# Moving the gate of a mixer's output projection onto its weights, and splitting its last half by columns

## The reference

```python
mix = jnp.concatenate([h_m, h_a], axis=-1) @ w_out[l]
x = x + gate1 * mix
hn2 = rms_norm(x, g_norm2[l]) * (1.0 + scale2) + shift2
ffn = hierarchical_moe(hn2, ...)      # route to 2 of 32 experts, SwiGLU, d_expert 512
x = x + gate2 * ffn
```

## Time and profile before

| what | us |
|---|---|
| median of 3 runs | 1333.73 (1332.79 to 1334.61) |
| the profiled execution | 1333.06 |
| its span from first to last instruction | 1331.1 |
| PE busy in the span | 1307.8 (98%), 7862 matmuls |
| DVE busy | 791.4 (59%) |
| ACT busy | 566.0 (43%) |
| POOL busy | 33.7 (3%), 55 instructions |
| DMA | 371.83 MB, mean 279 GB/s |
| granted TensorE clock, mean over the span | 0.997 of full |

### The profile page before, as it was taken

The page is one execution under the profiler, slowest core; times in us unless marked ns, Lnnn a source line. Parts: engine busy times, 40 slices in busy tenths (PEclk is TensorE's granted clock), DMA queues, the critical chain, the costliest instruction groups (busy, mean ns, idle before and its releaser), DMA issues.

```text
span 1331.1 us, 19341 instructions
## 1 busy us (share of the span) xinstructions
PE 1307.8 (98%) x7862; PEld 970.2 (73%) x7862; DVE 791.4 (59%) x1397; ACT 566.0 (43%) x859; POOL 33.7 (3%) x55
## 2 busy tenths in 40 slices
PE   8999999999999999999999999999999999999997
PEld 8988789999887997999987888754444544444442
DVE  5755598888986655898896877743222222223213
ACT  5344545655546576666655746531111111111112
POOL 0200010000001000100010000000000000000000
PEclk9999999999999999999999999999999999999998
DMA  9467286767585742555765573599999999999995
GB/s 354 165 222 259 103 301 218 237 216 252 196 290 176 236 147 95 170 191 187 253 226 190 206 253 127 190 398 412 427 429 427 429 428 428 428 426 429 426 423 204
DMA packets 113373, 371.83 MB, mean 279 GB/s; under 512 B 4604, under 2 KB 64284, under 8 KB 100368
## 3 DMA queue, kind: packets, MB, share of 16 engines
q1 hardware_dynamic: 105648, 344.07, 67.1%
q0 software_dynamic: 7648, 26.72, 5.7%
HBM read 369.71 MB, written 1.05 MB: 279 GB/s over the span
## 4 chain that ended last, share of the span: by engine, by line
PE 86%; DMA 7%; DVE 4%; ACT 2%; SPq 1%; issue 1%; DVEq 0%; ACTq 0%
PE ps L673 15%; PE ps L1588 14%; PE ps L633 9%; PE ps L634 9%; PE ps L635 9%; PE ps L1611 7%; PE ps L1570 4%; PE ps L650 4%; PE ps L652 3%; PE ps L651 3%; DMA arena<-in_w_expert_gate_dram 3%; DMA arena<-in_w_expert_down_dram 3%; PE ps L1617 2%; DVE w_low L568 1%; DMA const<-in_const_dram 1%; PE ps L1262 1%
## 5 line engine op out<-in xcount | busy, mean ns | idle before, releaser
L568 DVE TENSOR_TENSOR w_low<-ring,w_high 128x1024 fp32r<-128x1024 f32 x264 | 311.5, 1221 | 98.4 <-ACT w_high L560 97.6
L560 ACT ACTIVATE w_high<-ring 128x1024 fp32r<-128x1024 f32 x264 | 264.9, 1052 | 177.9 <-PE ps L673 82.8
L633 PE MATMUL ps<-h_high,w_high 128*128 128x256 f32 x1088 | 310.4, 285 | 1.6 <-DVE h_low L472 1.4
L634 PE MATMUL ps<-h_low,w_high 128*128 128x256 f32 x1088 | 307.8, 283 | 0.0
L635 PE MATMUL ps<-h_high,w_low 128*128 128x256 f32 x1088 | 307.7, 283 | 0.0
L633 PEld LDWEIGHTS ps<-h_high,w_high 128*128 128x128 f32 x1088 | 208.6, 192 | 7.2 <-issue 5.2
L634 PEld LDWEIGHTS ps<-h_low,w_high 128*128 128x128 f32 x1088 | 208.7, 192 | 0.0
L635 PEld LDWEIGHTS ps<-h_high,w_low 128*128 128x128 f32 x1088 | 208.6, 192 | 0.0
L1588 PE MATMUL ps<-ring,arena 128*64 128x512 f32 x592 | 176.6, 594 | 2.2 <-DMA arena<-in_w_expert_gate_dram 1.7
L1588 PEld LDWEIGHTS ps<-ring,arena 128*64 128x64 f32 x592 | 56.3, 137 | 111.6 <-issue 111.5
L673 PE MATMUL ps<-w_high,h_high 128*128 128x512 f32 x304 | 95.0, 394 | 1.0 <-DVE arena L2373 0.9
(11 more groups left out here) (402 smaller groups left out, 1682.5 us busy)
## 6 DMA issues: line engine op xcount, KB each, us to landing
ring<-in_ffn_w_up_dram SPq DMA_DIRECT2D x44, 1024.0 KB, 7.6
ring<-in_w_expert_gate_dram SPq DMA_DIRECT2D x19, 2048.0 KB, 23.1
ring<-in_w_expert_up_dram SPq DMA_DIRECT2D x18, 2048.0 KB, 19.6
ring<-in_w_expert_down_dram SPq DMA_DIRECT2D x17, 2048.0 KB, 24.2
ring<-in_ret_w_in_dram SPq DMA_DIRECT2D x11, 2048.0 KB, 8.2
arena<-in_w_expert_up_dram SPq DMA_DIRECT2D x11, 2048.0 KB, 25.7
ring<-in_ffn_w_down_dram SPq DMA_DIRECT2D x10, 2048.0 KB, 8.3
arena<-in_w_expert_gate_dram SPq DMA_DIRECT2D x9, 2048.0 KB, 21.1
```

The source lines that it names most:

```text
L560: nc.scalar.activation(hi, raw, ACT.Copy).then_inc(hi_done, 1)
L568: last = eng.tensor_tensor(lo, raw, hi.bitcast(F32), ALU.subtract)
L633: nc.tensor.matmul(o, hi, hTh[:, k, :], start=(k == 0 if whole else n == 0), stop=False, skip_group_check=not whole)
L634: nc.tensor.matmul(o, hi, hTl[:, k, :], start=False, stop=False, skip_group_check=not whole)
```

## The change

The gate is multiplied into `w_out` in its ring slots by GpSimd, eight multiplications of 128x1024, in place, float32. Two of them (`pool_done`) release the high split of each half of `mix_out` on ACT. The residual is then one addition PSUM plus x per column half. In the last half of `mix_out`, tile 1 is multiplied by column halves: all six matmuls of column half 0, a signal (`tile0_mm` once more), then the six of column half 1. The scratch tile `gtmp` goes. The semaphore `ada_zero` is renamed and shared.

```diff
@@ split_high
             if m >= 2:
                 act.wait_ge(wide_mm, (m - 1) if i is None else i * per + (m - 1))
+            if phase == "mix_out":
+                act.wait_ge(pool_done, 2 + h + 1)
@@
+        def by_columns(pe, h, w):
+
+            for half in range(2):
+                for kc in range(2):
+                    hi, lo = (s[:, 2 * (h % 4) + kc, P:T] for s in (hTh, hTl))
+                    for a, b, c in ((hi, 0, 0), (hi, 1, 1), (lo, 0, 2)):
+                        cols = slice(kc * D + half * C, kc * D + (half + 1) * C)
+                        last = nc.tensor.matmul(ps[:, 6 + half, :], a, w[b][:, cols], start=False, stop=(kc == 1 and c == 2))
+                if half == 0:
+                    last.then_inc(tile0_mm, 1)
+            return last
@@ project
                 for t in range(NT):
                     if t and middle is not None:
                         middle(h)
+                    if t and phase == "mix_out" and h == n - 1:
+                        last = by_columns(pe, h, w)
+                        continue
@@
-        def gated_residual(link, g, bank, tmp, tiles):
-
-            for t in tiles:
-                for half in range(2):
-                    last = nc.vector.tensor_tensor(tmp[:, t, half * C:(half + 1) * C], ps[:, bank + 2 * t + half, :],
-                                                   gates[:, g, half * C:(half + 1) * C], ALU.mult)
-            link(last)
-            for t in tiles:
-                nc.vector.tensor_tensor(x[:, t, :], x[:, t, :], tmp[:, t, :], ALU.add).then_inc(x_new, 2)
@@ end of GpSimd's program
+            pool.wait_ge(ada_gate, 4)
+            for n in phases["mix_out"]:
+                slot = units[n][1]
+                pool.wait_ge(ring_in[slot], arrivals(n))
+                for k in range(4):
+                    gated = nc.gpsimd.tensor_tensor(tall[slot][:, k, :], tall[slot][:, k, :], gates[:, 0, :], ALU.mult)
+                    if k % 2:
+                        gated.then_inc(pool_done, 1)
@@ VectorE's program
             for t in range(NT):
-                if t == 0:
-                    dve.wait_ge(tile0_mm, len(PROJECTIONS))
-                    wide_done(dve, n_halves - 1)
-                else:
-                    wide_done(dve, n_halves)
-                dve.wait_ge(ada_gate, 4)
-                gated_residual(link, 0, 4, gtmp, (t,))
+                for half in range(2):
+                    if t == 0 and half == 0:
+                        dve.wait_ge(tile0_mm, len(PROJECTIONS))
+                        wide_done(dve, n_halves - 1)
+                    elif t == 1:
+                        dve.wait_ge(*((wide_mm, n_halves) if half else (tile0_mm, len(PROJECTIONS) + 1)))
+                    xs = x[:, t, half * C:(half + 1) * C]
+                    nc.vector.tensor_tensor(xs, ps[:, 4 + 2 * t + half, :], xs, ALU.add).then_inc(x_new, 1)
```

More of the change, by code:

```diff
@@ L747, in build @@
         perm_in = sem("perm_in")
-        ada_used, ada_ev, ada_zero, ada_mods, ada_ms, mods_in, ada_gsum, ada_gate, ada_c, bias_in = (
-            sem("ada_" + n) for n in ("used", "evicted", "zero", "mods", "mods_row", "mods_in", "gate_sum", "gate", "c",
+        ada_used, ada_ev, pool_done, ada_mods, ada_ms, mods_in, ada_gsum, ada_gate, ada_c, bias_in = (
+            sem("ada_" + n) for n in ("used", "evicted", "pool_done", "mods", "mods_row", "mods_in", "gate_sum", "gate", "c",
                                       "bias_in"))
@@ L836, in build @@
         selw = carve(896, NT, P)
-        gtmp = carve(1408, NT, D)
         xg = carve(1408, KD, P)
@@ L1067, in _ @@
             pool.wait_ge(x_new, update(2))
-            nc.gpsimd.memset(w8, 0.0).then_inc(ada_zero, 1)
-            pool.wait_ge(ada_zero, 2)
+            nc.gpsimd.memset(w8, 0.0).then_inc(pool_done, 1)
+            pool.wait_ge(pool_done, 2)
             pool.dma_start(w8[:, :, 0:8], A["w_in_2"][0].rearrange("(k p) n -> p k n", p=P)[:, :, 4 * LH * LDH:4 * LH * LDH + 8])\
@@ L1757, in _ @@
             vg_group(3, ACT.Silu, False)
-            act.wait_ge(ada_zero, 1)
+            act.wait_ge(pool_done, 1)
             act.wait_ge(small_in, 32)
@@ L2142, in _ @@
             link = Link(dve, dve_chain)
-            nc.vector.memset(hT[:, 0, :], 0.0).then_inc(ada_zero, 1)
+            nc.vector.memset(hT[:, 0, :], 0.0).then_inc(pool_done, 1)
             split_low(dve, "ret_qk", 0)
```

## The result

| | before | changed |
|---|---|---|
| median of 6 runs, us | 1334.11 (1332.79 to 1336.42) | 1343.49 (1342.79 to 1344.45) |
| span of the profiled execution, us | 1331.1 | 1341.7 |
| DVE busy, us | 791.4 | 801.5 |
| POOL busy, us | 33.7 | 54.7 |

The ratio is 1.0074, 95% interval 1.0064 to 1.0084: the changed kernel is slower by 8.5 to 11.2 us, 9.4 by the medians and 10.6 by the two spans. The forecast was +5.8 us and 1339.5, with a range up to 1343.8.

A forecast was written before the change was run, and what follows sets the result against it. The end was taken to be set by the expert-weight stream's restart, delayed by the PE, DVE, ACT chain before it. Terms -0.4 + 6.2 = +5.8 us on the median 1333.73 gave 1339.5 us, range 1332.9 to 1343.8.

The forecast's parts named there:

- The 2.0 us of tile 1: Residual at the end of `mix_out`: tile 1's x ready 2.0 us sooner, but nobody waits for it, so no gain.
- Rival C: DVE and POOL don't exclude each other; only the 0.4 us wait at the first transpose goes: 1333.3 us, chance 0.24.
- B: DVE and POOL exclude each other, but the room takes it: 0 to 2.7 us late, 1333.5 to 1336, chance 0.12.
- D: Faster: all DVE time removed would be on the path, 2.5 us, giving 1331.3 us; chance 0.04.
- Part 1, -0.4 us,: Residual at the mixer's end: tile 0's x comes sooner, PE's wait goes, and the end gains -0.4 us.
- The wait of 0.4 us: At PE's first transpose: its weight load waited 0.4 us for DVE's tile 0 addition; this would go whole.
- Part 4, +6.2 us,: POOL's multiplications and DVE's work in `mix_out` hold each other off, making the kernel +6.2 us slower.
- The middle of two orders: POOL against DVE's low splits: the middle of alternate turns (8 us) and DVE keeping its turn (4 us), +6.2 us.
- the walk: Step-by-step timing of DVE's low splits, halves 11 to 13, against POOL's 2.4 us operations: PE stands 8 us in all.
- The split of half 13 has 3 us of room.: POOL's last two operations meet half 13's split and the gated rows behind it: between 0 and 1 us more.

The follow-up runs named there:

- e1: The changed kernel without GpSimd's eight multiplications and ACT's wait for them, gate left out: 1332.85 us against 1333.25 for the kernel before, ratio 0.9998.
- e7: The changed kernel without GpSimd's multiplications (gate left out) and with the last half of the projection in the old order: 1333.37 us against 1333.36 before.
- e3: The kernel before plus sixteen GpSimd memsets of 128x1024 into a spare row, no multiplication: 1333.11 us against 1333.25, ratio 1.0000.
- e2: The kernel before plus only GpSimd's eight multiplications and the waits for them, old gated residual kept: 1343.94 us against 1333.25, ratio 1.0082.
- e4: The changed kernel with each GpSimd multiplication cut into four of 128x256, 32 in all: 1338.26 us against 1333.25 before, ratio 1.0036.
- e6: The changed kernel with GpSimd multiplying only the second weight tile, the other half's gate left out: 1340.10 us against 1333.36 before, ratio 1.0050.
- e5: The changed kernel with GpSimd multiplying only the first weight tile, the other half's gate left out: 1337.03 us against 1333.36 before, ratio 1.0026.

## Why the prediction was wrong in size

**What held.** The end is set by the weight stream's restart, and a delay ahead of it goes through whole: 10.6 us at the restart, 10.6 in the span. The 2.0 us of tile 1 were hidden: with x ready that much sooner e1 gains 0.25 us in all, and e7 shows it for the 0.6 us of the column halves. POOL's operation is 2.4 us (2372 ns the shortest, 2420 ns the median). That this figure was met is in part luck: it was two reads at the memset's 1.2 ns for each element, and a memset of the full 1024 elements takes 0.97 us (e3), 0.94 ns each, by which two reads would have come to 1.9 us. ACT did not wait for `pool_done`: POOL was done with the first tile at 808.9 and with the second at 830.6, and ACT came to the first high split of `mix_out` at 837.6. POOL's multiplications and DVE's low splits and scalings exclude each other, and all of the loss comes from POOL's multiplications (e1, e2). Rival C falls with the 3.42 us of the low split, B with the restart at 864.35, D with e1.

**Part 1, -0.4 us,** was 0.25 (e1). The wait of 0.4 us in the earlier trace rows was not all an excess: the first transposes come 862.41 - 853.77 = 8.64 us behind the restart before and 8.49 in e1, and the router's products are 0.25 us sooner.

**The step that failed is the size of Part 4, +6.2 us,** which is 10.9 (e2). Three steps of it:

- *The middle of two orders.* I averaged alternate turns (8 us) with DVE keeping its turn between its two pieces (4 us). The rows show that DVE does not keep it: wherever POOL had an operation left, it ran between the two pieces (the second pair here, and in e2, e4 and e6). The first pair started behind POOL's last operation on that tile and met no other; the pairs take 4.55 and 4.52 us. Taking the end of alternate turns alone would have given +8, 1341.3.
- *One-input operations were left out of the walk.* I read from the earlier trace rows that a scaling from SBUF uses two paths, and then walked only the two-input low splits past POOL. In the changed kernel the scalings account for more of DVE's lost time than the splits: (3.23 - 0.55) + (4.61 - 0.55) + (1.88 - 0.16) = 8.5 us in two pairs and one single, against (4.55 - 2.36) + (4.52 - 2.36) = 4.3 us in four.
- *"The split of half 13 has 3 us of room."* It had, for its own collision. By then POOL was done (830.6) and its low split ran undisturbed, but it started at 832.2 in place of 819.7, behind the held scalings. PE stood for half 13 as well (1.9 us), and for the gated rows after it (0.9 us).

In the walk half 12 itself was put at 8 us late; it is 5.6, because its first piece got in 0.05 us ahead of POOL's first operation. In e2, where POOL was first, it is 7.7, as walked. The missing part came behind it: the walk put 0 to 1 us there, and it is 4.9 in the changed kernel and 3.2 in e2. DVE lost 12.8 us in these nine instructions and the restart came 10.6 us late, so the room in the chain took some 2 us.

## What to carry to other kernels

"POOL is idle" is not spare capacity while DVE works from SBUF to SBUF. Here every DVE instruction with two inputs in SBUF, and every scaling from SBUF to SBUF, that came while a multiplication ran waited for it to end, however small it was (reductions, reciprocals and copies out of PSUM did not). So count these in the stretch, the small ones too, and charge each with what is left of POOL's operation. If the work must be there, shorter POOL operations help: they halved the loss here, but lasted longer in all and reached new victims. Before DVE time is moved, look for who waits for it: here 2 us less on DVE were worth 0.25.

## What the runs showed of the hardware that I had not expected

- A DVE scaling of 8 elements took 1.88 us beside a multiplication on POOL, and 0.54 beside a memset, in place of 0.16 (changed kernel, e3).
- POOL's memset of 128x1024 took 0.97 us (e3), less than the 1.2 us scaled from 128x256. Multiplications of 128x256 took 0.72 us at the least, 2.9 us for 1024 elements, against 2.4 in one piece (e4).
- A stall of PE of 1.8 us (e5) or 3.9 us (changed kernel) was followed by a stretch at half of the full clock, 1.2 of 2.4 GHz; in e5 it began 1.3 us after PE had gone on. In the changed kernel it began with the first matmul after the stall and lasted 3.3 us. But stalls of 1.9 us before half 13, in the changed kernel and in e6, were followed by no such stretch, so these runs give no rule.
- Reductions, reciprocals and copies out of PSUM ran beside POOL's multiplications in their usual time (0.41, 0.15 and 0.55 us in the changed kernel), while scalings from SBUF and instructions with two inputs in SBUF were held.
